# Chunked attention on one core: the second head's normalisation on GpSimd, its copy out of PSUM on VectorE

## The chip, the cores and the metric

The kernel runs on one core of a Trainium2 chip. The metric is the device time of one execution in microseconds, lower is better. Of the core's engines, TensorE (PE) multiplies matrices and transposes by a matmul, VectorE (DVE) and ScalarE (ACT) work on tiles of 128 partitions in SBUF or in the matmul banks (PSUM), GpSimd (POOL) works on SBUF, and SyncE (SP) issues most DMAs. They run unsynchronised but for semaphores.

## The reference

A first block of two layers and a second block of one, on 512 tokens of width 1024, in float32. Each layer has two feed-forward parts around a mixer. The odd layer's mixer is the one touched: attention in bands of chunks beside a pooling of several scales.

```python
def _chunk_band_attention(q, k, v, q_gain, k_gain, rel_bias):
    '''Each chunk attends to itself and LEFT_CHUNKS previous chunks. (B,S,512) each -> (B,S,512).'''
    ...
    scores = jnp.einsum('bclhd,bckhd->bhclk', q.astype(f32), kb.astype(f32)) * (ATT_HEAD_DIM ** -0.5)
    ...
    scores = jnp.where(valid[None, None, :, None, :], scores + bias[None, :, None], -jnp.inf)
    probs = jax.nn.softmax(scores, axis=-1)
    out = jnp.einsum('bhclk,bckhd->bclhd', probs, vb.astype(f32))
```

There are 8 heads of 64, chunks of 64 tokens and 8 chunks to the left, so with 512 tokens a query sees all keys up to the end of its own chunk.

## The kernel before, in words

Most of the time goes into dense products whose weights are split into a high and a low part (ScalarE copies the high part, line 242, VectorE subtracts the low one, line 248) and multiplied in three matmuls (lines 294 to 296 and their like). Each stage is written by hand: for every engine a block with its instructions in order, and semaphores between them. Between two stages all engines meet at a barrier. GpSimd clears the semaphores of stages gone by behind such a barrier (line 164), before it enters its own block of the next stage, if it has one.

`chunk_attend` (line 2530 on) is one such stage. It goes through n = 16 steps, a step being a pair of heads c (the first on partitions 0 to 63, the second on 64 to 127 of the operands) and a block t of 128 queries. The width of a step is (t + 1) x 128 keys. The steps of the first pair stand in the order t = 0, 1, 2, 3, those of the other three pairs in the order 3, 1, 2, 0: widths 512, 256, 384, 128, which makes a round of four steps. For each step and head:

- TensorE makes the scores in PSUM banks 0 to 3 (`scores`, line 2568).
- VectorE adds the bias, writes them to the tile `ca_sc` (three buffers) and takes the maximum (line 2667), and negates the maxima of both heads (line 2671).
- ScalarE takes the exponential in place and its sum (line 2641).
- VectorE takes the reciprocal of both sums (line 2675) and multiplies each head's exponentials by its own (line 2679). Semaphore `normed` counts these.
- TensorE transposes the probabilities in blocks of 128 into bank 4 (first head) or 5 (second head) (`turn`, line 2577).
- ScalarE copies each bank to the tile `ca_pt` (two buffers, line 2636). Semaphore `copied` counts these.
- TensorE multiplies with the values (`weigh`, line 2589).

The engines run ahead of each other: in its turn k TensorE does the scores of step k, the turns of step k - 2 and the weighting of step k - 3. A bank is turned into again when its copy of the step before is done. VectorE in its turn k does the maxima of step k, then the reciprocal and products of step k - 1. GpSimd has no block in this stage. At the end of each pair of heads its output goes out in two parts (lines 2652 and 2697), and in the last turns the pooling's products (line 2599) and the first matmuls of the next stage follow (line 354 on).

Of the kernel before, what the change touches and what calls it, by code (L numbers as in the profile page):

```python
# [19 lines left out]
ALU = mybir.AluOpType  # L20
ACT = mybir.ActivationFunctionType
# [2509 lines left out]
def chunk_attend(co, QK, V, BIAS, M, POOLED, PW, cols, nxt):  # L2531
# [7 lines left out]
    nc = co.nc  # L2539
    order = [(0, 1, 2, 3)] + 3 * [(3, 1, 2, 0)]  # L2540
    steps = [(c, t) for c in range(4) for t in order[c]]
    n = len(steps)
    with ExitStack() as ctx:
        SC = co.sb("ca_sc", [P, 3, 2, S], ctx=ctx)
        PT = co.sb("ca_pt", [P, 2, 2, S], ctx=ctx)
        ST = co.sb("ca_st", [P, 3, 4, 2], ctx=ctx)
        T = [co.RS, co.SS]
        (scored, biased, negated, powered, inverted, normed, turned, copied, weighted, out_hi, out_lo, pooled, scaled,
         rounded, parted) = (co.sem(f"ca_{s}") for s in (
            "scored", "biased", "negated", "powered", "inverted", "normed", "turned", "copied", "weighted", "out_hi",  # L2550
            "out_lo", "pooled", "scaled", "rounded", "parted"))
        block = ctx.enter_context(co.block())
        width = lambda k: (steps[k][1] + 1) * P

        @block.sync
        def _(sp):
            co.load_second(sp, nxt)

        @block.tensor
        def _(pe):  # L2560
            def scores(k):
                c, t = steps[k]
                w = width(k)
                if k >= 2:
                    pe.wait_ge(biased, 2 * (k - 2) + 2)
                for s in range(2):
                    r = HD * s
                    nc.tensor.matmul(co.PS[:, 2 * (k % 2) + s, 0:w], QK[r:r + HD, c, t * P:(t + 1) * P],
                                     QK[r:r + HD, 4 + c, 0:w], start=True, stop=True).then_inc(scored, 1)

            def turn(k):
                for s in range(2):
                    pe.wait_ge(normed, 2 * k + s + 1)
                    if k >= 1:
                        pe.wait_ge(copied, 2 * (k - 1) + s + 1)
                    for j in range(steps[k][1] + 1):
                        m = nc.tensor.transpose(co.PS[:, 4 + s, j * P:(j + 1) * P], SC[:, k % 3, s, j * P:(j + 1) * P],
                                                co.ident)
                    m.then_inc(turned, 1)

            def weigh(k):
                c, t = steps[k]
                pe.wait_ge(copied, 2 * k + 2)
                if k % TT == 0 and c >= 2:
                    pe.wait_ge(out_lo, c - 1)
                for j in range(t + 1):
                    for s in range(2):
                        h = 2 * c + s
                        m = nc.tensor.matmul(co.PS[HD * s:HD * s + HD, 6 + c % 2, t * P:(t + 1) * P],
                                             V[:, j, h * HD:(h + 1) * HD], PT[:, k % 2, s, j * P:(j + 1) * P],  # L2590
                                             start=j == 0, stop=j == t)
                m.then_inc(weighted, 1)

            def pooled_half(g):
                if g >= 2:
                    pe.wait_ge(scaled, g - 1)
                else:
                    pe.wait_ge(biased, 2 * n)
                nc.tensor.matmul(co.PS[:, 2 + g % 2, :], PW[:, g, :], POOLED[:, g, :], start=True, stop=True).then_inc(pooled, 1)
            def bank_read(pe, bank):  # L2600
                if bank == 2:
                    pe.wait_ge(scaled, 3)
                else:
                    pe.wait_ge(biased, 2 * n)
            for k in range(n + 3):
                if k < n:
                    scores(k)
                if 2 <= k < n + 2:
                    turn(k - 2)
                if k >= n + 1:  # L2610
                    for g in (2 * (k - n - 1), 2 * (k - n - 1) + 1):
                        pooled_half(g)
                if k >= 3:
                    weigh(k - 3)
                if k == n + 1:
                    pe.wait_ge(out_lo, 3)
                    co.begin_unit(pe, nxt, 0, (0, 1, 2), bank_read, last=False)
            pe.wait_ge(parted, 2)
            co.begin_unit(pe, nxt, 0, (4, 5), first=False, last=False)
            pe.wait_ge(parted, 4)  # L2620
            co.begin_unit(pe, nxt, 0, (6, 7), first=False, last=False)
            pe.wait_ge(out_lo, 4)
            co.begin_unit(pe, nxt, 0, (3,), first=False)
            for j in range(1, RAW - 1):
                co.begin_unit(pe, nxt, j, range(DC), bank_read)

        @block.scalar
        def _(act):
            for k in range(n + 3):
                if 2 <= k < n + 2:  # L2630
                    w = width(k - 2)
                    if k >= 4:
                        act.wait_ge(weighted, k - 3)
                    for s in range(2):
                        act.wait_ge(turned, 2 * (k - 2) + s + 1)
                        nc.scalar.activation(PT[:, k % 2, s, 0:w], co.PS[:, 4 + s, 0:w], ACT.Copy).then_inc(copied, 1)
                if k < n:
                    w = width(k)
                    act.wait_ge(negated, k + 1)
                    for s in range(2):  # L2640
                        nc.scalar.activation(SC[:, k % 3, s, 0:w], SC[:, k % 3, s, 0:w], ACT.Exp,
                                             bias=ST[:, k % 3, 1, s:s + 1], accum_out=ST[:, k % 3, 2, s:s + 1]).then_inc(powered, 1)
                if k == SPLIT_STEP:
                    co.split_hi(act, nxt, 0, 1)
                if k >= n + 1:
                    for g in (2 * (k - n - 1), 2 * (k - n - 1) + 1):
                        act.wait_ge(scaled, g + 1)
                        nc.scalar.activation(M[0][:, 4 + g, :], T[g % 2][:], ACT.Copy).then_inc(rounded, 1)
                if k >= 3 and (k - 3) % TT == TT - 1:
                    c = steps[k - 3][0]  # L2650
                    act.wait_ge(weighted, k - 2)
                    nc.scalar.activation(M[0][:, c, :], co.PS[:, 6 + c % 2, :], ACT.Copy).then_inc(out_hi, 1)
            for j in range(SPLIT, RAW):
                co.split_hi(act, nxt, 0, j)

        @block.vector
        def _(dve):
            v = nc.vector
            for k in range(n + 3):
                if k < n:  # L2660
                    c, t = steps[k]
                    w = width(k)
# [9 lines left out]
                if 1 <= k < n + 1:  # L2672
                    b = (k - 1) % 3
                    dve.wait_ge(powered, 2 * k)
                    v.reciprocal(ST[:, b, 3, :], ST[:, b, 2, :]).then_inc(inverted, 1)
                    dve.wait_ge(inverted, k)
                    w = width(k - 1)
                    for s in range(2):
                        v.tensor_scalar(SC[:, b, s, 0:w], SC[:, b, s, 0:w], ST[:, b, 3, s:s + 1], None,
                                        ALU.mult).then_inc(normed, 1)  # L2680
                if k == SPLIT_STEP + 1:
                    co.split_lo(dve, nxt, 0, 1)
                if k >= n + 1:
# [723 lines left out]
```

## Time and profile before

| | |
|---|---|
| median of 3 runs | 2734.49 us (2733.83 to 2734.65) |
| profiled execution | 2734.27 us, span from first to last instruction 2732.5 us |
| TensorE busy | 2696.5 us, 99% of the span |
| VectorE busy | 1402.7 us, 51% |
| ScalarE busy | 963.4 us, 35% |
| GpSimd busy | 208.1 us, 8% |
| mean granted TensorE clock | 0.999 |

The stage of the change begins at the barrier at about 1413.5 us and its last steps end at about 1456 us. TensorE's busy time counts from the start of a matmul to an end that is modelled, and consecutive matmuls overlap in it; the distance from one start to the next says what a matmul costs in a dense row. "PEld" is its weight loader, which may be idle while a matmul runs.

### The profile page before, as it was taken

To read this page: it belongs to the slowest core of one execution; us is meant where nothing else is said; L and a number is where in the kernel's file an instruction comes from. 1 tells how busy PE (TensorE), PEld (TensorE's weight loads), DVE (VectorE), ACT (ScalarE), POOL (GpSimd) and SP (SyncE) were. 2 spreads that over 40 slices of the span, in tenths; PEclk is the share of its full clock that TensorE was granted. 3 is DMA by queue.
4 is the path that set the end of the run, shared out by engine and by line. 5 is a ranking of instruction groups with operands and counts; after the bars stand their busy time and mean duration, and the time that the engine had idled before them with its cause. 6 is when DMAs were issued, how large, how long until landed. Compare 5 with 4: busy or idle time off the path is not lost. (4 is left out here: it accounts for less than half of the span.)

```text
span 2732.5 us, 33671 instructions
## 1 busy us (share of the span) xinstructions
PE 2696.5 (99%) x12904; PEld 2209.0 (81%) x12904; DVE 1402.7 (51%) x1806; ACT 963.4 (35%) x1346; POOL 208.1 (8%) x220
## 2 busy tenths in 40 slices
PE   8999999999999999999999999999999999999998
PEld 7888888788888888888877888888888777788887
DVE  6676236754443254442585544423998535633334
ACT  5433224643332233322245333222223642433213
POOL 2001013010000000000301000000000000300003
PEclk9999999999999999999999999999999999999999
DMA  4334236132233222232311222333442024222331
GB/s 161 123 129 170 97 108 185 51 138 99 94 104 108 81 92 100 92 111 91 118 62 62 100 92 100 112 111 106 149 135 78 33 73 139 81 93 99 104 106 52
DMA packets 77680, 282.74 MB, mean 103 GB/s; under 512 B 10240, under 2 KB 10880, under 8 KB 76816
## 3 DMA queue, kind: packets, MB, share of 16 engines
q1 hardware_dynamic: 66672, 248.50, 26.9%
q0 software_dynamic: 6304, 26.65, 3.0%
q10 hardware_dynamic: 4608, 6.30, 0.9%
q8 instruction: 62, 1.02, 0.2%
q14 instruction: 34, 0.28, 0.0%
HBM read 261.22 MB, written 13.89 MB: 101 GB/s over the span
## 5 line engine op out<-in xcount | busy, mean ns | idle before, releaser
L248 DVE TENSOR_TENSOR wl<-raw,wh 128x1024 fp32r<-128x1024 f32 (+3 forms) x435 | 562.7, 1293 | 1062.2 <-ACT wh L242 1061.1
L242 ACT ACTIVATE wh<-raw 128x1024 fp32r<-128x1024 f32 (+3 forms) x436 | 480.0, 1101 | 1093.2 <-PE PS L296 905.7
L294 PE MATMUL PS<-Hh,wl 128*128 128x512 f32 x2154 | 843.2, 391 | 1.7 <-DVEq L1493 0.5
L295 PE MATMUL PS<-Hh,wh 128*128 128x512 f32 x2154 | 838.2, 389 | 0.0
L296 PE MATMUL PS<-Hl,wh 128*128 128x512 f32 x2154 | 838.2, 389 | 0.0
L294 PEld LDWEIGHTS PS<-Hh,wl 128*128 128x128 f32 x2154 | 404.4, 188 | 89.9 <-issue 4.5
L295 PEld LDWEIGHTS PS<-Hh,wh 128*128 128x128 f32 x2154 | 404.4, 188 | 85.0 <-issue 1.9
L296 PEld LDWEIGHTS PS<-Hl,wh 128*128 128x128 f32 x2154 | 404.3, 188 | 83.9
L294 PE MATMUL PS<-ffn_gh,wl 128*128 128x512 f32 x880 | 342.7, 389 | 0.0
L296 PE MATMUL PS<-ffn_gl,wh 128*128 128x512 f32 x880 | 342.3, 389 | 0.0
L295 PE MATMUL PS<-ffn_gh,wh 128*128 128x512 f32 x880 | 342.3, 389 | 0.0
L294 PEld LDWEIGHTS PS<-ffn_gh,wl 128*128 128x128 f32 x880 | 165.2, 188 | 34.7 <-issue 0.2
L296 PEld LDWEIGHTS PS<-ffn_gl,wh 128*128 128x128 f32 x880 | 165.2, 188 | 34.4
L295 PEld LDWEIGHTS PS<-ffn_gh,wh 128*128 128x128 f32 x880 | 165.2, 188 | 34.2 <-issue 0.2
L1009 DVE TENSOR_TENSOR ffn_gl<-ffn_t,ffn_gh 128x512 f32 (+1 forms) x110 | 76.4, 694 | 93.1 <-ACT ffn_gh L972 93.1
L966 ACT ACTIVATE ffn_sg<-ffn_sg 128x512 f32<-128x512 f32 x88 | 55.7, 633 | 160.8 <-DVE ffn_sg L998 160.8
L972 ACT ACTIVATE ffn_gh<-ffn_t 128x512 f32 (+1 forms) x110 | 69.5, 632 | 109.9 <-DVE ffn_t L1003 77.3
L354 PE MATMUL PS<-Hh,wl 128*128 128x512 f32 x222 | 90.8, 409 | 10.5 <-DVE Hl L1229 8.0
L596 POOL TENSOR_TENSOR SS<-SS,ffn_sg 128x512 f32<-128x512 f32 x24 | 30.7, 1281 | 797.1 <-ACT ffn_sg L578 797.1
L355 PE MATMUL PS<-Hh,wh 128*128 128x512 f32 x222 | 87.4, 394 | 0.0
L356 PE MATMUL PS<-Hl,wh 128*128 128x512 f32 x222 | 87.3, 393 | 0.0
L2923 DVE SCALAR_TENSOR_TENSOR X<-conv_u,cols,X 128x512 f32<-128x512 f32 x124 | 85.0, 744 | 0.0
(495 smaller groups left out, 2533.9 us busy)
## 6 DMA issues: line engine op xcount, KB each, us to landing
raw<-in_gu SPq DMA_DIRECT2D x220, 512.0 KB, 3.6
raw<-in_dn SPq DMA_DIRECT2D x80, 704.0 KB, 4.0
raw<-in_hin SPq DMA_DIRECT2D x44, 512.0 KB, 3.6
raw<-in_oin SPq DMA_DIRECT2D x16, 512.0 KB, 3.6
raw<-in_hin_gate SPq DMA_DIRECT2D x16, 512.0 KB, 3.6
X<-QKV ACTq DMA_DIRECT2D x96, 64.0 KB, 2.0
kept_x<-X POOLq DMA_DIRECT2D x16, 256.0 KB, 3.6
raw<-in_eout SPq DMA_DIRECT2D x8, 512.0 KB, 3.7
```

The costliest lines, as they stand in the source:

```text
L242: self.nc.scalar.activation(self.wh[j % SPLIT][:, 0:kw], self.raw[j][:, 0:kw], ACT.Copy).then_inc(self.hi_ready, 1)
L248: self.nc.vector.tensor_sub(self.wl[j % SPLIT][:, 0:kw], self.raw[j][:, 0:kw], self.wh[j % SPLIT][:, 0:kw].bitcast(F32)).then_inc(self.lo_ ...
L294: self.nc.tensor.matmul(out, wl, xh[:, at, :], start=first, stop=False)
L295: self.nc.tensor.matmul(out, wh, xh[:, at, :], start=False, stop=False)
L296: done = self.nc.tensor.matmul(out, wh, xl[:, at, :], start=False, stop=last)
L354: self.nc.tensor.matmul(out, wl, xh[:, at, :], start=start, stop=False)
L355: self.nc.tensor.matmul(out, wh, xh[:, at, :], start=False, stop=False)
L356: done = self.nc.tensor.matmul(out, wh, xl[:, at, :], start=False, stop=stop)
L966: nc.scalar.activation(SG[:, c], SG[:, c], ACT.Silu).then_inc(gated, 1)
L972: nc.scalar.activation(one(Gh, n), T[:, c], ACT.Copy).then_inc(rounded, 1)
L1009: nc.vector.tensor_sub(one(Gl, n), T[:, c], one(Gh, n).bitcast(F32)).then_inc(g_ready, 1)
L2923: self.co.nc.vector.scalar_tensor_tensor(self.CV[:, n, :], self.U[:, n, tap:tap + S], self.co.cols[:, k:k + 1], self.CV[:, n, :], ALU.mult ...
```

## The change

In `chunk_attend`, three pieces of work of the second head change hands:

- the product of its exponentials with the reciprocal sum goes from VectorE (line 2679) to GpSimd, which gets a block in this stage with 16 such instructions;
- the copy of its turned probabilities from bank 5 to `ca_pt` goes from ScalarE (line 2636) to VectorE, where it stands behind the first head's product;
- `normed` and `copied` become two semaphores each, one per head, so the stage has 17 semaphores where it had 15.

```diff
+        normed = [co.sem(f"ca_normed{s}") for s in range(2)]
+        copied = [co.sem(f"ca_copied{s}") for s in range(2)]
...
+        @block.gpsimd
+        def _(pool):
+            for k in range(n):
+                b, w = k % 3, width(k)
+                pool.wait_ge(inverted, k + 1)
+                nc.gpsimd.tensor_scalar(SC[:, b, 1, 0:w], SC[:, b, 1, 0:w], ST[:, b, 3, 1:2], None,
+                                        ALU.mult).then_inc(normed[1], 1)
...
             def turn(k):
                 for s in range(2):
-                    pe.wait_ge(normed, 2 * k + s + 1)
+                    pe.wait_ge(normed[s], k + 1)
                     if k >= 1:
-                        pe.wait_ge(copied, 2 * (k - 1) + s + 1)
+                        pe.wait_ge(copied[s], k)
...
             def weigh(k):
-                pe.wait_ge(copied, 2 * k + 2)
+                for s in range(2):
+                    pe.wait_ge(copied[s], k + 1)
...
         def _(act):
-                    for s in range(2):
-                        act.wait_ge(turned, 2 * (k - 2) + s + 1)
-                        nc.scalar.activation(PT[:, k % 2, s, 0:w], co.PS[:, 4 + s, 0:w], ACT.Copy).then_inc(copied, 1)
+                    act.wait_ge(turned, 2 * (k - 2) + 1)
+                    nc.scalar.activation(PT[:, k % 2, 0, 0:w], co.PS[:, 4, 0:w], ACT.Copy).then_inc(copied[0], 1)
...
         def _(dve):
-                    for s in range(2):
-                        v.tensor_scalar(SC[:, b, s, 0:w], SC[:, b, s, 0:w], ST[:, b, 3, s:s + 1], None,
-                                        ALU.mult).then_inc(normed, 1)
+                    v.tensor_scalar(SC[:, b, 0, 0:w], SC[:, b, 0, 0:w], ST[:, b, 3, 0:1], None,
+                                    ALU.mult).then_inc(normed[0], 1)
+                if 2 <= k < n + 2:
+                    w = width(k - 2)
+                    if k >= 4:
+                        dve.wait_ge(weighted, k - 3)
+                    dve.wait_ge(turned, 2 * (k - 2) + 2)
+                    v.tensor_copy(PT[:, k % 2, 1, 0:w], co.PS[:, 5, 0:w]).then_inc(copied[1], 1)
```

Line numbers in the rows of order are each kernel's own. VectorE's queue before, in the first pair of heads, from the negated maxima of one step to those of the next (2667 are the maxima and their read-out, 2671 the negation, 2675 the reciprocal, 2679 the two heads' products):

```order
L2671 TENSOR_SCALAR ca_st<-ca_st 128x2
L2675 RECIPROCAL ca_st<-ca_st 128x2
L2679 TENSOR_SCALAR ca_sc<-ca_sc,ca_st 128x384 x2
L2667 ISA ca_sc,ca_st<-PS,BIAS 128x512
L2667 ISA ca_st 128x1
L2667 ISA ca_sc,ca_st<-PS,BIAS 128x512
L2667 ISA ca_st 128x1
L2671 TENSOR_SCALAR ca_st<-ca_st 128x2
```

The same place on VectorE after the change (2677, 2681, 2685 and 2688 answer to 2667, 2671, 2675 and 2679; 2695 is the copy out of bank 5):

```order
L2681 TENSOR_SCALAR ca_st<-ca_st 128x2
L2685 RECIPROCAL ca_st<-ca_st 128x2
L2688 TENSOR_SCALAR ca_sc<-ca_sc,ca_st 128x384
L2695 COPY ca_pt<-PS 128x256
L2677 ISA ca_sc,ca_st<-PS,BIAS 128x512
L2677 ISA ca_st 128x1
L2677 ISA ca_sc,ca_st<-PS,BIAS 128x512
L2677 ISA ca_st 128x1
L2681 TENSOR_SCALAR ca_st<-ca_st 128x2
```

One product of a step is left, and the copy of the step before it (256 keys beside 384) stands between that product and the maxima of the step after.

GpSimd's queue at the entry of the stage, as a difference (L164 are the semaphore clears, L2561 the entry of its new block, L1047 that of the next stage):

```order
-L164 ISA x63
+L164 ISA x48
+L2561 UNCONDITIONAL_BRANCH
+L2566 TENSOR_SCALAR ca_sc<-ca_sc,ca_st 128x128
+L2566 TENSOR_SCALAR ca_sc<-ca_sc,ca_st 128x256
+L2566 TENSOR_SCALAR ca_sc<-ca_sc,ca_st 128x384
+L2566 TENSOR_SCALAR ca_sc<-ca_sc,ca_st 128x512 x2
```

Before, 48 clears stood behind the barrier at the stage's beginning and 15 behind the one at its end, with nothing between them. Now the 48 stand ahead of the 16 products, and 17 follow at the end.

## Rows read from the trace of the kernel before

**Rows 1.** Busy time by stretch, inside the stage; the first line names the columns

```profile
core 0: us, PE busy (x) PEld busy (x) DVE busy (x) ACT busy (x) POOL busy (x), PEclk, DMA share, GB/s
1430.00:1440.00 10.00, 9.85 (x85) 6.00 (x82) 8.49 (x35) 7.96 (x27) 0.00 (x0) 1.00 0.00 0
```

**Rows 2.** Waits in the stage: who for whom, us in total, times, longest

```profile
PEld PS L2577 <- DVE ca_sc L2679: 8.7, 15, 1.3
```

**Rows 3.** Timeline of TensorE, one round: start us, us, operation, count, idle before

```profile
1429.47 1.13 PE L2568 MATMUL PS<-QK 64*128 64x512 f32 x4
1430.53 0.88 PE L2577 MATMUL PS<-ident,ca_sc 128*128 128x128 f32 x6
1431.34 0.66 PE L2589 MATMUL PS<-ca_pt,V 128*64 128x128 f32 x8
1431.92 0.70 PE L2568 MATMUL PS<-QK 64*128 64x256 f32 x4
1432.70 0.53 PE L2577 MATMUL PS<-ident,ca_sc 128*128 128x128 f32 x2
1433.15 0.88 PE L2589 MATMUL PS<-ca_pt,V 128*64 128x128 f32 x12
1433.96 0.92 PE L2568 MATMUL PS<-QK 64*128 64x384 f32 x4
1434.81 1.09 PE L2577 MATMUL PS<-ident,ca_sc 128*128 128x128 f32 x8
1435.83 0.44 PE L2589 MATMUL PS<-ca_pt,V 128*64 128x128 f32 x4
1436.20 0.49 PE L2568 MATMUL PS<-QK 64*128 64x128 f32 x4
1436.77 0.70 PE L2577 MATMUL PS<-ident,ca_sc 128*128 128x128 f32 x4
1437.41 1.09 PE L2589 MATMUL PS<-ca_pt,V 128*64 128x128 f32 x16
1438.43 1.13 PE L2568 MATMUL PS<-QK 64*128 64x512 f32 x4
```

**Rows 4.** Groups by form: VectorE's products, count, busy us, mean ns, idle before

```profile
L2679 DVE TENSOR_SCALAR ca_sc<-ca_sc,ca_st 128x512 f32<-128x512 f32 x8 | 3.5, 484 | 0.1
...
L2679 DVE TENSOR_SCALAR ca_sc<-ca_sc,ca_st 128x128 f32<-128x128 f32 x8 | 1.9, 284 | 0.1
```

**Rows 5.** Lines by source: VectorE's copies out of PSUM, ns least/median/most

```profile
L3035 DVE COPY QKV<-PS x2: 681/687/693, 2102.9 to 2103.5; 128x512 f32<-128x512 f32 x2
...
L1539 DVE COPY AC<-PS x1: 183/183/183, 464.0 to 464.0; 128x32 f32<-128x32 f32 x1
```

**Rows 6.** Lines by source: GpSimd's tensor_scalar, ns least/median/most

```profile
L2411 POOL TENSOR_SCALAR POOLED<-POOLED x4: 1450/1452/1469, 1343.8 to 1369.5; 128x496 f32<-128x496 f32 x4
...
L1320 POOL TENSOR_SCALAR SZ<-SZ x7: 287/289/732, 428.7 to 435.1; 128x32 f32<-128x32 f32 x7
```

**Rows 7.** Timelines of VectorE and GpSimd elsewhere, two places where they meet

```profile
575.59 1.22 DVE L248 TENSOR_TENSOR wl<-raw,wh 128x1024 fp32r<-128x1024 f32 x1 [1.23 <-ACT wh L242]
...
575.59 2.37 POOL L596 TENSOR_TENSOR SS<-SS,res_sq 128x512 f32<-128x512 f32 x1
...
1371.07 1.30 POOL L2412 TENSOR_TENSOR POOLED<-POOLED,UU 128x512 f32<-128x512 f32 x1
...
1371.42 2.02 DVE L248 TENSOR_TENSOR wl<-raw,wh 128x1024 fp32r<-128x1024 f32 x1
```

**Rows 8.** Timeline of VectorE in the round: reciprocals at two steps, one pair of products

```profile
1432.16 0.16 DVE L2675 RECIPROCAL ca_st<-ca_st 128x2 f32<-128x2 f32 x1
...
1433.84 0.17 DVE L2675 RECIPROCAL ca_st<-ca_st 128x2 f32<-128x2 f32 x1
1434.04 0.89 DVE L2679 TENSOR_SCALAR ca_sc<-ca_sc,ca_st 128x512 f32<-128x512 f32 x2
```

**Rows 9.** The stage's start: GpSimd's semaphore clears, and TensorE's first turns

```profile
L164 POOLq EVENT_SEMAPHORE_RANGE_CLEAR  x48: 44/44/44, 1413.6 to 1417.2; - x48
...
1416.36 0.53 PE L2577 MATMUL PS<-ident,ca_sc 128*128 128x128 f32 x2 [0.73 <-DVE ca_sc L2679]
```

More of the change, by code:

```diff
@@ L2547, in chunk_attend @@
         T = [co.RS, co.SS]
-        (scored, biased, negated, powered, inverted, normed, turned, copied, weighted, out_hi, out_lo, pooled, scaled,
+        (scored, biased, negated, powered, inverted, turned, weighted, out_hi, out_lo, pooled, scaled,
          rounded, parted) = (co.sem(f"ca_{s}") for s in (
-            "scored", "biased", "negated", "powered", "inverted", "normed", "turned", "copied", "weighted", "out_hi",
+            "scored", "biased", "negated", "powered", "inverted", "turned", "weighted", "out_hi",
             "out_lo", "pooled", "scaled", "rounded", "parted"))
+        normed = [co.sem(f"ca_normed{s}") for s in range(2)]
+        copied = [co.sem(f"ca_copied{s}") for s in range(2)]
         block = ctx.enter_context(co.block())
```

## The prediction

> **What bounds the kernel now.** I read the page's busy shares first: TensorE 99% of the span, VectorE 51%, ScalarE 35%, GpSimd 8%. The change lives in one stage of some 45 us, so I looked next at that stage by windows [rows 1]: in 10 us TensorE is busy 9.85, VectorE 8.49, ScalarE 7.96, GpSimd 0, at the full granted clock of 2.4 GHz (1.00). Three engines are nearly full, and the busy TensorE is a modelled figure, so it does not say who leads. The waits do [rows 2]: 8.7 us of idle on TensorE's weight loader end with VectorE's products (line 2679), longest 1.3 us. Most of that idle lies under matmuls still running; what truly stops TensorE must be counted from the spacing of its groups.
>
> That is the third view, the timeline of one round of four steps (widths 512, 256, 384, 128 keys) [rows 3]. The round takes 1438.43 - 1429.47 = 8.96 us. Unwaited costs, start to next start: scores 1.06 (512) and 0.85 (384), so 0.21 per 128 keys and 0.64 and 0.42 for the narrow ones; turns 0.81 for 6 transposes and 1.02 for 8, so 0.59 for 4 and 0.37 for 2; weighting 0.58, 0.81, 0.37, 1.02 for 8, 12, 4, 16 matmuls. Sum: 2.97 + 2.79 + 2.78 = 8.54. So TensorE waits 0.42 in the round; it is the bound, and VectorE's chain, scores to product, follows closely. Three such rounds hold 1.3 us of waits; the same count of the timeline's other steps gives about 1.2 us before step 4 and 0.4 in steps 4 to 7, and some 0.5 at the end: about 3.4 us of real waiting in the stage. No relief of the other engines can give back more.
>
> **The change, part by part.** (a) ScalarE loses 16 copies of the second head's turned scores. It is not what TensorE waits for (0.42 a round ends with VectorE's products), so I price it at nothing; the exponentials can start earlier, which VectorE, itself the later one, does not use. Bounds: 0 to -1.3 us.
>
> (b) VectorE loses one product per step and gains one copy out of PSUM. The products took 484 ns at 512 keys and 284 at 128 [rows 4], 0.48 + 0.42 + 0.35 + 0.28 = 1.53 us a round. The copy at 512 columns is 687 ns and at 32 columns 183 [rows 5], 1.05 ns a column: 0.69 + 0.55 + 0.42 + 0.28 = 1.94. VectorE's share of a round rises from 0.849 x 8.96 = 7.6 to 8.0 of 8.96 us: fuller, not yet the bound by sum. But the copy is a new wait in VectorE's row of work: it stands after the remaining product and before the next step's reductions, and holds them until TensorE has turned the second head. TensorE in turn may not turn the second head of the next step until that copy has emptied the bank.
>
> (c) GpSimd takes the second head's product. A tensor_scalar there took 1450 ns at 496 columns and 287 at 32 when undisturbed [rows 6], so 2.51 ns a column against 0.52 on VectorE: 1.49 us at 512 keys, 1.17, 0.85 and 0.53 at 384, 256 and 128. The row takes a number as its factor and the new instruction a column of values; VectorE pays about 60 ns for that, so I take the rows' durations and keep +0.3 us for the upper end, and -0.2 for the lower.
>
> (d) Both products are released by the same reciprocal. What happens when VectorE and GpSimd want SBUF together is in [rows 7]: released in the same instant, 575.59, VectorE's took 1.22 us, its usual time, and GpSimd's took 2.37, where 1.30 is what such a one takes alone (third row): it ran after VectorE's, with some 0.13 of its start beside it. Started second, VectorE is the one who pays: GpSimd at 1371.07 for 1.30, VectorE at 1371.42 for 2.02 instead of 1.22. Those are VectorE instructions with two SBUF operands; none in this trace shows VectorE's one-operand product beside GpSimd. Bounds for the hold: none to the whole product, and I take the whole, with VectorE first, as in the nearest row. The Trainium skill, page "SBUF — State Buffer", section "Who interferes with whom", says that a VectorE tensor_scalar in its two-port form and any GpSimd instruction exclude each other for the whole instruction, whoever issued first. By that rule the sum is the 3.3 us below, without it 2.6; the trace agrees in so far as [rows 7] show exclusion and [rows 4] a product at 0.52 ns a column, half of the copy's 1.05, as a form with two ports would have it.
>
> Now the second head's product at 512 keys, from the reciprocal's start. Before: 0.20 + 0.89 for the pair [rows 8] = 1.09. After: 0.20 + 0.48 held + 1.36 = 2.04. In the round shown the reciprocal starts at 1433.84, so the product comes at 1435.88, with 0.06 to the release 1435.94; TensorE wants it at 1434.81 + 0.50 = 1435.31. It waits 0.63, where it had 0.32 to spare. At 128 keys: reciprocal at 1432.16, VectorE's product 0.20 + 0.20, then the copy of the 384-key step 0.55 and 0.06: the bank is free at 1433.17, wanted at 1432.70 + 0.19 = 1432.89, a wait of 0.28. At 384 keys the product (1.66 after its reciprocal) still hides.
>
> Each stall also moves what follows, so I stepped through all 16 steps with these durations, each engine in its new order and each wait honoured. On the order before, this walk gives a round of 8.90 (the trace: 8.96); on the new order 9.60, with TensorE waiting 0.49 for the 512-key product, 0.10 for the 256-key one, and 0.44 at the 128-key step (0.30 of it for the copy). So +0.7 a round.
>
> (e) The start. GpSimd clears 48 semaphores after the barrier, until 1417.2 [rows 9], and only then enters the new block; idle before, this cost nobody. Its first product starts at about 1417.4 and ends at 1417.95. TensorE turned the second head of step 0 at 1416.56 (0.2 into the group at 1416.36) and will at 1418.04, 1.5 us later. As it waited for VectorE shortly after anyway, 1.0 us is left at the scores of step 4. Bounds: 0.2 (were the clears free) to 1.5.
>
> Sum by the walk: start +1.0; steps 4 to 7, where wide products follow each other, +0.9; two rounds +0.7 each; the tail, which waits for the same pooled products as before, about 0: **+3.3 us**. The walk runs 0.06 a round short, so I say +3.5. The profiled execution took 2734.27 us around a span of 2732.5; the median of the runs is 2734.49, 0.2 more. 2734.49 + 3.5 = **2738.0 us**. Behind the stage TensorE runs without gaps, so the shift is kept whole.
>
> **The rivals.**
> A. It gets faster or stays: the relieved ScalarE and the half-relieved pair of products let TensorE run dry of waits. For it: the 8.7 us of loader idle that end with VectorE's products, and TensorE at 98% in the stage, where only 3.4 us can be had. Against: that product is not removed but made 0.95 us later at 512 keys. It would give up to -2 us: 2732.5 to 2735. Chance 0.12.
>
> B. GpSimd wins the port. If its product is already streaming when VectorE's is issued, the first head waits for the second: VectorE's product starts 1.5 us later, its copy, reductions and next reciprocal with it. It decides from the point at which GpSimd starts before VectorE; the walk with that order loses 2.5 us by step 4 and 3.5 us in each round, +15 us: 2749.5. For it: VectorE at 1371.42 [rows 7]. Against: the tie at 575.59 went to VectorE, and here VectorE starts 0.03 us after its own reciprocal. The same page's rule, that issue order decides who blocks, would give this time if GpSimd is the earlier; the trace shows no such pair of starts here. Chance 0.07.
>
> C. GpSimd's product costs more with a column as factor, or its start is later than I think: +0.3 us a product makes +5.3, +0.5 makes +6.7 (the walk), and a start 1 us later adds 1.0: 2739.5 to 2743. Chance 0.23.
>
> D. GpSimd's product is as quick as VectorE's in effect. The copy alone then costs +1.6: 2736. Chance 0.10, inside the main case's side of zero.
>
> Main case, +1.8 to +5: chance 0.48.
>
> **How the numbers follow.** The time is the main case's. The range: below it A leaves some 0.1 out, above it B and a little of C; 2735.3 to 2743. From 0.2% (5.5 us) a change of this kernel can be told from none. Faster by that much would need more than the 3.4 us that the stage holds: 0.02. Slower by it needs C's upper half or B: 0.25. The rest, 0.73, is within it, most of it on the slow side.
>
> **What would show it.** GpSimd in the stage: 16 tensor_scalar instructions, the first at 1417.3 to 1417.7, of some 1.85 us at 512 keys when the hold is counted in their time (1.5 if there is none), VectorE's own product staying at 0.48. TensorE's round 9.6 us, the second head's turns released by GpSimd at 512 keys and by the copy at the 128-key step, and the scores of step 4 near 1420.2. VectorE's copies 0.69 us at 512. I am wrong if the round stays at 9.0 (then the product hides and A or D holds), if VectorE's products grow beyond 1 us (B), or if GpSimd's exceed 2.1 us (C).

## The result, and the profile after

The changed kernel takes 2739.01 us (median of 20 runs, 2737.77 to 2743.78) against 2734.53 us of the kernel before (20 runs): +4.5 us, ratio 1.0017, 95% interval 1.0011 to 1.0023. The forecast was 2738.0 with a range to 2743.0. The profiled execution took 2738.76 us around a span of 2737.0.

The stage can be measured in the trace, from its first scores to the last of the next stage's products that wait for it. I measure every kernel below in that way, since the profiled executions reach this stage at times up to 1.4 us apart (1412.93 to 1414.36) for reasons that lie in other stages. Stations, in us from the stage's first scores:

| | scores of step 4 | of step 8 | of step 12 | first pooled product | end | stage against before |
|---|---|---|---|---|---|---|
| before | 5.52 | 15.82 | 24.78 | 35.98 | 46.39 | |
| after | 7.67 | 19.51 | 29.33 | 41.39 | 51.81 | +5.42 |

The stage lost 5.42 us. The profiled execution reached it at 1412.93 where before's did at 1413.65, and another 0.2 us was made up behind it, so its whole time is only 4.5 more. By stations: +2.15 up to step 4, +1.54 in steps 4 to 7, +0.86 in the round to step 12, +0.86 to the first pooled product, +0.01 behind it.

TensorE's timeline of the changed kernel, the start and one whole round, answers to [rows 3] (start us, us, operation, count, and the idle time before with what ended it; the round in [rows 3] began at 1429.47):

```profile
1412.93 1.98 PE L2578 MATMUL PS<-QK 64*128 64x128 f32 x12 [0.30 <-PEq L180]
1415.64 0.33 PE L2587 MATMUL PS<-ident,ca_sc 128*128 128x128 f32 x1 [0.73 <-DVE ca_sc L2688]
1417.39 0.33 PE L2587 MATMUL PS<-ident,ca_sc 128*128 128x128 f32 x1 [1.42 <-POOL ca_sc L2566]
1417.64 1.35 PE L2578 MATMUL PS<-QK 64*128 64x512 f32 x4
1418.92 1.11 PE L2587 MATMUL PS<-ident,ca_sc 128*128 128x128 f32 x4
...
1420.59 1.73 PE L2578 MATMUL PS<-QK 64*128 64x512 f32 x4
1422.25 0.88 PE L2587 MATMUL PS<-ident,ca_sc 128*128 128x128 f32 x6
...
1432.44 1.13 PE L2578 MATMUL PS<-QK 64*128 64x512 f32 x4
...
1434.89 0.70 PE L2578 MATMUL PS<-QK 64*128 64x256 f32 x4
1435.66 0.33 PE L2587 MATMUL PS<-ident,ca_sc 128*128 128x128 f32 x1
1436.22 0.30 PE L2587 MATMUL PS<-ident,ca_sc 128*128 128x128 f32 x1 [0.23 <-DVE ca_pt L2695]
1436.45 0.88 PE L2600 MATMUL PS<-ca_pt,V 128*64 128x128 f32 x12
...
1438.10 0.66 PE L2587 MATMUL PS<-ident,ca_sc 128*128 128x128 f32 x4
1439.03 0.66 PE L2587 MATMUL PS<-ident,ca_sc 128*128 128x128 f32 x4 [0.27 <-POOL ca_sc L2566]
1439.62 0.44 PE L2600 MATMUL PS<-ca_pt,V 128*64 128x128 f32 x4
...
1440.41 0.89 PE L2587 MATMUL PS<-ident,ca_sc 128*128 128x128 f32 x4
1441.23 1.09 PE L2600 MATMUL PS<-ca_pt,V 128*64 128x128 f32 x16
1442.25 1.13 PE L2578 MATMUL PS<-QK 64*128 64x512 f32 x4
```

The round is 1442.25 - 1432.44 = 9.81 us, 9.82 by the stations, where it was 8.96. Two idle times are printed, but the spacing shows four places. With the unwaited costs of the prediction (turns 0.37, 0.59, 1.02 for 2, 4, 8 transposes, scores of 256 keys 0.64): turns of the 128-key step 1436.45 - 1435.66 = 0.79, so 0.42 waited; turns at 512 keys 1439.62 - 1438.10 = 1.52, so 0.50; at 256 keys 1441.23 - 1440.41 = 0.82, so 0.23; and 0.13 behind the scores at 1434.89. Together 1.28, where the round before had 0.42.

At the start there is something else. Four scores of 512 keys take 1.06 us from start to start in a dense row; here they take 1418.92 - 1417.64 = 1.28 and 1422.25 - 1420.59 = 1.66. Busy time by stretch, with the granted clock as the column behind POOL, tells why; the last row answers to [rows 1]:

```profile
core 0: us, PE busy (x) PEld busy (x) DVE busy (x) ACT busy (x) POOL busy (x), PEclk, DMA share, GB/s
1412.00:1414.00 2.00, 1.57 (x16) 1.00 (x14) 1.06 (x6) 1.48 (x2) 0.00 (x0) 1.00 0.06 20
1414.00:1416.00 2.00, 1.23 (x5) 0.43 (x5) 1.85 (x11) 1.99 (x9) 0.00 (x0) 1.00 0.69 244
1416.00:1418.00 2.00, 0.61 (x3) 0.44 (x5) 1.37 (x8) 1.53 (x7) 1.34 (x2) 1.00 0.01 2
1418.00:1420.00 2.00, 2.00 (x10) 0.75 (x6) 0.91 (x4) 0.43 (x2) 0.24 (x1) 0.61 0.00 0
1420.00:1422.00 2.00, 2.00 (x9) 0.77 (x8) 1.43 (x6) 1.35 (x4) 1.19 (x1) 0.54 0.00 0
1422.00:1424.00 2.00, 2.00 (x20) 1.35 (x18) 1.50 (x6) 0.69 (x3) 0.28 (x1) 1.00 0.00 0
1430.00:1440.00 10.00, 9.42 (x86) 5.64 (x82) 8.41 (x35) 6.87 (x22) 5.29 (x5) 1.00 0.00 0
```

TensorE's granted clock fell to its lower level, 1.2 GHz, for 2 x (0.39 + 0.46) / 0.5 = 3.4 us. In a busy-share view this is invisible: TensorE counts 2.00 of 2.00 while it does half the work. In the kernel before it is 1.00 in the same stretch (rows in the last section), and here it is again from 1422 on.

The waits in the stage (who for whom, us in total, times, longest), where [rows 2] had 8.7 us of the loader's idle ended by VectorE:

```profile
PEld PS L2587 <- POOL ca_sc L2566: 5.4, 9, 1.6
...
PEld PS L2587 <- DVE ca_sc L2688: 4.1, 6, 1.3
```

The loader's wait has changed its address, and GpSimd now ends the larger part. Durations by form in the stage (count, busy us, mean ns), answering to [rows 4 to 6]:

```profile
L2566 POOL TENSOR_SCALAR ca_sc<-ca_sc,ca_st 128x512 f32<-128x512 f32 x4 | 7.4, 1856 | 4.1 <-DVE ca_st L2685 4.0
L2566 POOL TENSOR_SCALAR ca_sc<-ca_sc,ca_st 128x384 f32<-128x384 f32 x4 | 5.9, 1470 | 4.8 <-DVE ca_st L2685 4.8
L2566 POOL TENSOR_SCALAR ca_sc<-ca_sc,ca_st 128x256 f32<-128x256 f32 x4 | 4.2, 1041 | 3.4 <-DVE ca_st L2685 3.4
L2566 POOL TENSOR_SCALAR ca_sc<-ca_sc,ca_st 128x128 f32<-128x128 f32 x4 | 2.8, 690 | 49.2 <-remote 44.9 <-DVE ca_st L2685 4.3
...
L2695 DVE COPY ca_pt<-PS 128x512 f32<-128x512 f32 x4 | 2.7, 686 | 0.2 <-PE PS L2587 0.2
...
L2688 DVE TENSOR_SCALAR ca_sc<-ca_sc,ca_st 128x512 f32<-128x512 f32 x4 | 1.9, 486 | 0.2
```

GpSimd needs 1.86 us at 512 keys, VectorE's product beside it is as long as it was (486 against 484 ns), and the copy takes 0.69. The means at 256 and 128 keys contain the first two products, which met VectorE's in another order or not at all (0.92 and 0.68 us); the later ones take 1.08 and 0.69.

### The profile page after: what moved, and what is told of

It is laid out like the page before. It is cut to its first block and busy times, and to the rows that moved or that the text cites. A ratio compares the mean times of both kernels' runs of the same rounds, so it can differ in the third digit from the quotient of the medians.

```text
span 2737.0 us, 33701 instructions
## 1 busy us (share of the span) xinstructions
PE 2698.7 (99%) x12904; PEld 2209.2 (81%) x12904; DVE 1404.3 (51%) x1806; ACT 959.0 (35%) x1330; POOL 228.3 (8%) x236
## 3 DMA queue, kind: packets, MB, share of 16 engines
q8 instruction: 62, 1.02, 0.2%
```

## The experiments

Three questions: what the start costs and why (clears, clock), what the copy and the product each cost in the steady rounds, and whether GpSimd's time is its own or held back by VectorE. Experiments 1 to 4 shared 33 runs of the kernel before (median 2734.40 us), 5 to 8 another 33 (2733.97); each ran 11 times. The edits are against the changed kernel. All stations together, in us as above; whether the clock falls is read from the profiled execution:

| | step 4 | step 8 | step 12 | pooled | end | stage | clock falls | median us | ratio (95%) |
|---|---|---|---|---|---|---|---|---|---|
| 1 product only | 7.52 | 19.52 | 29.27 | 41.47 | 51.87 | +5.48 | yes | 2739.18 | 1.0018 (1.0009-1.0027) |
| 2 copy only | 5.78 | 17.04 | 27.19 | 39.57 | 49.99 | +3.60 | no | 2737.63 | 1.0012 (1.0003-1.0021) |
| 3 kept busy | 6.74 | 18.25 | 28.06 | 40.14 | 50.55 | +4.16 | no | 2737.86 | 1.0012 (1.0003-1.0021) |
| 4 first two on VectorE | 5.78 | 17.09 | 26.91 | 39.36 | 49.77 | +3.38 | no | 2738.06 | 1.0012 (1.0003-1.0021) |
| 5 clears left out | 5.84 | 17.09 | 26.91 | 38.98 | 49.39 | +3.00 | no | 2737.08 | 1.0011 (1.0002-1.0020) |
| 6 after the first head | 7.45 | 19.99 | 30.21 | 42.74 | 53.15 | +6.76 | yes | 2739.94 | 1.0021 (1.0012-1.0030) |
| 7 no wide ones on GpSimd | 5.78 | 16.57 | 26.39 | 38.37 | 48.77 | +2.38 | no | 2736.54 | 1.0009 (1.0000-1.0018) |
| 8 narrow copies | 5.52 | 15.82 | 24.79 | 35.95 | 46.37 | -0.02 | no | 2734.03 | 0.9999 (0.9990-1.0008) |

The intervals of the ratios overlap for most pairs, so the separations rest on the stations, of one profiled execution each. How far these can be trusted shows where the code is equal: the round from step 8 to 12 is 9.81 or 9.82 us in the changed kernel and in experiments 3, 4 and 5. But from step 12 to the first pooled product experiment 4 takes 12.45 us and experiment 5, with the same instructions there, 12.08: the maxima of step 12 start 1.64 us after their scores and not 1.27, once, and nothing in that trace says why. So a difference of 0.4 us in one place can be chance. For the fall of the clock there is a second sign: of every run the mean granted clock is on record, and it is 0.998 in 6 of 20 runs of the changed kernel, 6 of 11 of experiment 1 and 7 of 11 of experiment 6, and in none of the 66 runs of the other six experiments.

**Experiment 1, the product alone.** ScalarE copies both heads again, GpSimd keeps the product.

```diff
         def _(act):
+                    act.wait_ge(turned, 2 * (k - 2) + 2)
+                    nc.scalar.activation(PT[:, k % 2, 1, 0:w], co.PS[:, 5, 0:w], ACT.Copy).then_inc(copied[1], 1)
         def _(dve):
-                    v.tensor_copy(PT[:, k % 2, 1, 0:w], co.PS[:, 5, 0:w]).then_inc(copied[1], 1)
```

> GpSimd makes all 16 second-head products as in the changed kernel, but ScalarE keeps copying both heads. Theory (three costs: GpSimd's late start with a drop of TensorE's clock behind it, the late 512-key product, the copy in VectorE's loop): the start and the wide products stay, the copy's part goes. Steps 0 to 3 cost +2.1 us as in the changed kernel, with a stretch of 3.4 us at half clock; rounds of about 9.6; in all +3.5 to +4.5 us against before. Rival (the copy on VectorE alone makes the loss, the product hides): +1 us or less, rounds at 9.0.

Measured: the stage is +5.48, as long as with both parts, and the median +4.8. The round is 9.75 (step 8 to 12), the start +2.00 with the clock down. The expectation was wrong in one part: the copy's share was to go (rounds of 9.6, +3.5 to +4.5), but the round is only 0.07 shorter with the copy back on ScalarE. At the 128-key step of the changed kernel the copy that empties the bank and GpSimd's product end at the same moment, 1436.08 and 1436.07:

```profile
1435.38 0.69 POOL L2566 TENSOR_SCALAR ca_sc<-ca_sc,ca_st 128x128 f32<-128x128 f32 x1 [2.07 <-DVE ca_st L2685]
1435.53 0.55 DVE L2695 COPY ca_pt<-PS 128x384 f32<-128x384 f32 x1
```

Without the copy TensorE still waits there for the product, 0.35 us for 0.42 by the spacing, and the 0.50 at 512 keys stays as it was. What ScalarE's relief is worth by itself this run does not say, since VectorE's load changes with it.

**Experiment 2, the copy alone.** Both products are VectorE's again, its copy stays.

```diff
-        @block.gpsimd
-        def _(pool):
...
+                    v.tensor_scalar(SC[:, b, 1, 0:w], SC[:, b, 1, 0:w], ST[:, b, 3, 1:2], None,
+                                    ALU.mult).then_inc(normed[1], 1)
```

> VectorE makes both products as before and also copies the second head out of PSUM; GpSimd has no block. Theory: no start cost and no clock drop (scores of step 4 at most 0.3 us late in the stage), but VectorE has 1.9 us more per round and becomes the bound: rounds of about 9.9 to 10.0, in all +2.5 to +3.5 us. Rival (GpSimd's product makes the whole loss, the copy hides in VectorE's idle): 0 to +0.5 us, rounds at 9.0.

Measured: +3.60 in the stage and +3.2 in the median, near the theory; the rival is out. The round is 10.15, longer than with both parts. Its timeline shows the place, the turns of the second head in the 128-key and the 256-key step:

```profile
1435.16 0.30 PE L2579 MATMUL PS<-ident,ca_sc 128*128 128x128 f32 x1 [0.42 <-DVE ca_pt L2689]
...
1439.97 0.41 PE L2579 MATMUL PS<-ident,ca_sc 128*128 128x128 f32 x2 [0.51 <-DVE ca_pt L2689]
```

Line 2689 is the copy: TensorE stands twice a round until VectorE has emptied the bank. VectorE is busy 9.33 us of these 10.15 and waits for scores in 0.54 of them; before, it was busy 7.73 of 8.96. This is no test of the prediction's rival D (+1.6), in which VectorE makes one product a step and not two. The two parts don't add. Alone they cost 0.79 (9.75) and 1.19 (10.15) a round, together 0.86: where VectorE must copy, GpSimd's product takes work off a full engine and gives 0.33 back.

**Experiment 3, TensorE kept busy.** Matmuls whose result nobody reads fill TensorE's wait for the first product of GpSimd; all else is the changed kernel.

```diff
             def turn(k):
                 for s in range(2):
+                    if k == 0 and s == 1:
+                        co.idle_products(7, 6)
                     pe.wait_ge(normed[s], k + 1)
```

> The changed kernel with six dummy 128x128 matmuls into an unused bank on TensorE, between the two turns of step 0, where it waits 1.4 us for GpSimd's first product. If the granted clock fell because of that wait: it stays at 1.00 all through the stage, the scores of step 4 come 1.1 us earlier, and the time is 0.9 to 1.2 us below the changed kernel's: +3.3 to +3.6 against before. Rival (the drop comes of something else, as GpSimd's or VectorE's load): the drop stays and the time is that of the changed kernel, +4.5.

Measured: the clock stays at 1.00 where it had fallen (windows with the columns of above),

```profile
1418.00:1420.00 2.00, 2.00 (x15) 0.90 (x14) 1.04 (x4) 0.79 (x3) 0.56 (x1) 1.00 0.00 0
1420.00:1422.00 2.00, 1.67 (x9) 0.60 (x7) 1.93 (x7) 1.20 (x3) 1.07 (x1) 1.00 0.00 0
```

and the stage is 5.42 - 4.16 = 1.26 us shorter, 0.93 of it by step 4 and 0.33 by step 8; from there on the stations run in parallel. The median, 2737.86, is 1.15 under the changed kernel's (1.0 if each is taken against the kernel before of its own set). So the idle TensorE brought the clock down, and that is worth 1.26 us here, not the 1.7 that 3.4 us at half speed would be; in part because TensorE, at full clock again, waits at other places (by its timeline 0.23 and 0.56 us at the turns of the 384-key step, step 2).

**Experiment 4, the first two products on VectorE.** GpSimd takes the second head from step 2 on.

```diff
+                if k >= 2:
+                    pool.wait_ge(inverted, k + 1)
+                    nc.gpsimd.tensor_scalar(SC[:, b, 1, 0:w], SC[:, b, 1, 0:w], ST[:, b, 3, 1:2], None,
+                                            ALU.mult).then_inc(normed[1], 1)
...
+                    if not ((k - 1) >= 2):
+                        v.tensor_scalar(SC[:, b, 1, 0:w], SC[:, b, 1, 0:w], ST[:, b, 3, 1:2], None,
+                                        ALU.mult).then_inc(normed[1], 1)
```

> The changed kernel, but VectorE makes the second head's products of steps 0 and 1; GpSimd begins with step 2. Theory (the start costs 2.1 us, about 1.0 by GpSimd's late entry behind its 48 semaphore clears and 1.1 by the clock that falls behind it): no wait at step 0, clock 1.00, scores of step 4 at most 0.3 us late, rounds unchanged at 9.8: +2.4 to +3.3 us against before. Rival (the start costs nothing that isn't paid anyway later): +4.5.

Measured: step 4 at 5.78, only 0.26 behind the kernel before, the clock at 1.00. Of the +2.15 at the start 1.89 is gone; the rounds are unmoved (9.82). The median is less clear than the stations, 2738.06 (2736.05 to 2738.72): +3.7, above the +2.4 to +3.3 expected. Of the stage's +3.38, 0.38 is the single delay behind step 12 named above; without it the stage would be +3.00, as in experiment 5.

**Experiment 5, the clears left out at this stage's entry.** GpSimd's 48 semaphore clears don't stand ahead of its first product but follow at the next stage's entry; all 16 products stay there.

```diff
-        co.begin()
+        co.begin(f.__name__ != "chunk_attend")
...
-    def begin(self):
+    def begin(self, clear=True):
+        if not clear:
+            self.stage_sems = StageSems()
+            return
```

> The changed kernel with GpSimd's 48 semaphore clears put off to the next stage's beginning, so that it can start the product of step 0 as soon as the reciprocal is there. If the clears are what holds the start: GpSimd's first product begins at its reciprocal (2.2 us into the stage's matmuls), TensorE waits under 0.4 us more at step 0 than before, clock 1.00, scores of step 4 at most 0.4 us late; stage 3.2 to 3.5 us longer than before, time +2.4 to +3.4. Rival (entering a block of its own is what costs, whatever stands ahead): start and clock as in the changed kernel, +4.5 to +5.4.

Measured: GpSimd's first product starts 2.44 us into the stage (which began at 1413.16) and not 3.73 (1416.66 - 1412.93), and it is released by the reciprocal:

```profile
1415.60 0.69 POOL L2569 TENSOR_SCALAR ca_sc<-ca_sc,ca_st 128x128 f32<-128x128 f32 x1 [43.71 <-DVE ca_st L2688]
```

Step 4 comes at 5.84, the clock does not fall; the stage is +3.00, a little under the 3.2 expected, and the median +3.1, as expected. So the queue of clears [rows 9] costs 1.83 us by step 4, its consequence on the clock included; GpSimd as the executor of the first two narrow products costs 0.06 more than VectorE (5.84 against 5.78).

**Experiment 6, GpSimd behind the first head.** Its product waits for VectorE's, so the two never overlap.

```diff
-                pool.wait_ge(inverted, k + 1)
+                pool.wait_ge(normed[0], k + 1)
```

> The changed kernel, but GpSimd waits for VectorE's product of the first head instead of the reciprocal, so that the two products never overlap. If in the changed kernel GpSimd is held for the whole of VectorE's product: its instructions now take 1.45 to 1.55 us at 512 keys instead of 1.86, and end no more than 0.15 us later; stage 0 to 0.8 us longer than the changed kernel's. Rival (the two share the memory at a lower rate): the instructions shrink too, but end 0.3 us or more later, VectorE's product at 0.49 gets shorter, and the stage grows by 1.3 us or more.

Measured: alone, the product takes

```profile
L2566 POOL TENSOR_SCALAR ca_sc<-ca_sc,ca_st 128x512 f32<-128x512 f32 x4 | 6.3, 1565 | 5.7 <-DVE ca_sc L2688 5.7
L2566 POOL TENSOR_SCALAR ca_sc<-ca_sc,ca_st 128x384 f32<-128x384 f32 x4 | 5.0, 1245 | 5.8 <-DVE ca_sc L2688 5.8
...
1436.54 0.61 POOL L2566 TENSOR_SCALAR ca_sc<-ca_sc,ca_st 128x128 f32<-128x128 f32 x1 [2.39 <-DVE ca_sc L2688]
```

and 0.93 us at 256 keys. That is 0.29, 0.22, 0.16 and 0.09 us less from 512 to 128 keys than in the changed kernel, where VectorE's products beside it take 0.49, 0.42, 0.35 and 0.29. At every width GpSimd loses VectorE's product less 0.20 us. Of these 0.20, 0.06 pass before GpSimd starts, and 0.14 of its own time lies beside VectorE's product: at 512 keys it ends 1.43 us behind VectorE's and takes 1.57 alone. The rest of VectorE's product it waits. The kernel is nevertheless slower, +1.34 in the stage and 10.22 a round. The 512-key product of the changed kernel and of this one, from the reciprocal on, first the changed kernel:

```profile
1436.87 0.16 DVE L2685 RECIPROCAL ca_st<-ca_st 128x2 f32<-128x2 f32 x1
1437.06 0.49 DVE L2688 TENSOR_SCALAR ca_sc<-ca_sc,ca_st 128x512 f32<-128x512 f32 x1
...
1437.12 1.86 POOL L2566 TENSOR_SCALAR ca_sc<-ca_sc,ca_st 128x512 f32<-128x512 f32 x1 [1.05 <-DVE ca_st L2685]
```

and experiment 6:

```profile
1437.70 0.16 DVE L2685 RECIPROCAL ca_st<-ca_st 128x2 f32<-128x2 f32 x1
1437.90 0.49 DVE L2688 TENSOR_SCALAR ca_sc<-ca_sc,ca_st 128x512 f32<-128x512 f32 x1
...
1438.48 1.56 POOL L2566 TENSOR_SCALAR ca_sc<-ca_sc,ca_st 128x512 f32<-128x512 f32 x1 [1.33 <-DVE ca_sc L2688]
```

The product ends 2.11 us after the reciprocal's start in the one and 1438.48 + 1.56 - 1437.70 = 2.34 in the other. So the overlap saves 0.23: the 0.14 beside VectorE, and 0.09 from the end of VectorE's product (1438.39) to GpSimd's start (1438.48), which the wait for its semaphore adds. Every GpSimd product later by that makes the round 0.40 longer. The theory is met in part: GpSimd's instructions shrink as it says, but they end 0.23 later and not within 0.15, and the stage's +1.34 is the rival's size. What the rival needs is missing: VectorE's product takes 0.49 alone as beside GpSimd's, so the two don't share at a lower rate.

**Experiment 7, no wide products on GpSimd.** It takes the second head only where there are fewer than 512 keys and from step 2 on; VectorE does the others.

```diff
+        gp = lambda k: k >= 2 and width(k) < S
...
+                if gp(k):
+                    pool.wait_ge(inverted, k + 1)
...
+                    if not gp(k - 1):
+                        v.tensor_scalar(SC[:, b, 1, 0:w], SC[:, b, 1, 0:w], ST[:, b, 3, 1:2], None,
+                                        ALU.mult).then_inc(normed_v, 1)
```

> GpSimd makes the second head's product only from step 2 on and only at widths under 512 keys; VectorE makes the others; VectorE copies the second head at every step. Against the run in which VectorE makes only the first two. If the 512-key product is what TensorE waits for besides the copy: about 0.5 us less in the stage, +2.4 to +3.1 against before. Rival (VectorE's load is the bound, as its copy alone costs 3.6 us in the stage): the product given back to VectorE lengthens it by 0.4 us at each of four steps, and the stage is as long as with the first two alone or longer.

Measured: +2.38 in the stage, 1.00 less than experiment 4, of which 0.52 comes in steps 4 to 7 and 0.47 behind step 12. Of the latter 0.38 is experiment 4's single delay; against experiment 5 the stage is 0.62 shorter, near the 0.5 expected. The round from step 8 is 9.82, unmoved: the wait at 512 keys is gone (its 8 transposes run as one group), but the one at 256 keys has grown from 0.23 to 0.57 by the spacing, and 0.16 has come in behind the scores ahead of it,

```profile
1437.51 0.44 PE L2595 MATMUL PS<-ident,ca_sc 128*128 128x128 f32 x2
1438.30 0.44 PE L2595 MATMUL PS<-ident,ca_sc 128*128 128x128 f32 x2 [0.35 <-POOL ca_sc L2569]
```

The wait at the 128-key step is 0.42 as before. So the wide product alone does not set the steady round; which loop of VectorE's copies and GpSimd's narrow products does, these rows don't settle. The 0.50 removed at one step came back at the next.

**Experiment 8, narrow copies only.** No GpSimd; VectorE does both products and copies the second head only at 128 and 256 keys, ScalarE at 384 and 512.

```diff
+        cv = lambda k: k >= 2 and width(k) <= 2 * P
...
+                    if not cv(k - 2):
+                        act.wait_ge(turned, 2 * (k - 2) + 2)
+                        nc.scalar.activation(PT[:, k % 2, 1, 0:w], co.PS[:, 5, 0:w], ACT.Copy).then_inc(copied[1], 1)
...
-                if 2 <= k < n + 2:
+                if 2 <= k < n + 2 and cv(k - 2):
```

> Both products on VectorE as before, GpSimd without a block; VectorE copies the second head out of PSUM only at 128 and 256 keys from step 2 on, ScalarE all else. If the copy costs by its length in VectorE's full queue: 0.28 and 0.42 us of copies where VectorE has idle time cost nothing, and the stage is that of before within 0.3 us. Rival (each copy costs by its place, since it makes VectorE wait for TensorE's turn): half of the loss of all copies, +1.5 to +2 us.

Measured: -0.02 in the stage, round 8.97, 2734.03 against 2733.97 us. Two of four copies a round on VectorE are free, and relieve ScalarE without any gain. So a copy does not cost by standing in that place. That the wide ones, 0.69 and 0.55 us in front of the next maxima, are what costs in experiment 2 is argued and not shown: no run has the wide ones alone, and it may be the sum that counts (VectorE is busy 8.17 of 8.97 us here, 9.33 of 10.15 there). Of all variants this is the only one whose stage is no longer than before's, and it is not faster either.

## Why the prediction was right, and where it was not

The direction, the place and the order of size were right: +3.5 forecast, +4.5 measured, inside the range. Step by step:

- **(a) ScalarE's relief is worth nothing**: right as far as it was tested. Experiment 8 relieves it of the narrow copies and gains nothing. Experiment 1 gives all copies back to it and the stage stays (+5.48 against +5.42), but VectorE's load changes with that.
- **(b) The copy is 0.69 us at 512 keys, and a new wait at the 128-key step**: right by rows; that wait was put at 0.44 and is 0.55, 0.42 at the turns and 0.13 behind the scores before them. The walk laid 0.30 of it to the copy. GpSimd's product ends at the same moment, and nearly all of the wait stays without the copy (experiment 1). Rival D's price of +1.6 was not tested: in experiment 2 (+3.60) VectorE has both products beside the copies, by the prediction's numbers 7.6 + 1.94 = 9.5 us of work in a round of 10.15.
- **(c) GpSimd's product**: 1.49, 1.17, 0.85 and 0.53 forecast, 1.57, 1.25, 0.93 and 0.61 measured alone (experiment 6). That is 0.08 us more at every width. The column as factor is the likely cause, like the 60 ns that VectorE pays for it, which the prediction kept for the upper end; no run changes the factor alone.
- **(d) The hold**: right. The row of the instruction came out at 1.86 against 1.85, with VectorE first and unhurt at 486 ns. The agreement hides two small errors of opposite sign: the product itself is 0.08 longer, and it starts 0.06 after VectorE's, which its row does not count. The 0.13 beside VectorE is right (0.14). GpSimd did run first in two places (rows in the last section): VectorE's product lost nothing in the one, and a small VectorE instruction 0.1 us in the other. The Trainium skill, page "SBUF — State Buffer", section "Who interferes with whom", has the later one blocked for the whole of the other's instruction. The trace agrees on who waits, less the 0.14 us at the start, but for the row at 1416.66, where VectorE's product came 0.18 us later and was not blocked.
- **Rounds**: +0.7 forecast, +0.86 measured, twice. The walk had 0.49 of waits at 512 keys, 0.10 at 256 and 0.44 at 128; measured are 0.50, 0.23 and 0.55 (0.42 + 0.13). The 0.08 of (c) goes the right way for this; no run isolates it.
- **Steps 4 to 7**: +0.9 forecast, +1.54 measured, of which experiment 3 gives 0.33 to the slow clock: 11.51 - 10.30 = 1.21 without it.
- **(e) The start**, the step that failed. The clears do hold the first product: it began 3.73 us into the stage, 3.75 was forecast (1417.4 - 1413.65), and experiment 5 shows that they alone do. The second head of step 0 was to be turned 1.5 us later and was, by 1.55 (4.46 us into the stage for 2.91), with TensorE idle for 1.42 before it. But "1.0 us is left at the scores of step 4" was 2.15. At full clock it is 1.22 (experiment 3); the other 0.93 is TensorE at 1.2 GHz for 3.4 us after that wait, of which the prediction has no word. It had read a clock of 1.00 in [rows 1] and carried it over to a stretch that the change itself thins out.
- **The tail**: 0 forecast, 0.01 measured.

In sum the walk's 3.3 stands against 4.16 at full clock (start +0.22, steps 4 to 7 +0.3, rounds +0.34), and the clock adds 1.26: 5.42. That is above the main case's +5. The whole time moved by +4.5 because the profiled execution reached the stage 0.72 us earlier and made up 0.2 behind it, where the prediction kept the shift whole; to that extent the closeness of the forecast is luck. The median of the 20 runs moved by +4.5 too, and the stage doesn't explain why; over the experiments the median moved between 0.8 us less and 0.3 more than the stage (+6.0 and +6.76 in the sixth, +3.7 and +3.38 in the fourth); the stations are from one execution each, and where the rest goes stays open.

The rivals: A (no slower) is out, since the whole interval of the ratio, 1.0011 to 1.0023, lies above 1. B did not happen. C's mechanism, a dearer product, is there at a quarter of its smallest size, 0.08 for 0.3. D is out by GpSimd's own 1.57 us for VectorE's 0.49, and by experiment 1, where the product alone costs 0.79 us a round.

Why no variant was faster: the 3.4 us of waits in the stage before lie in rounds of 8.96 us in which VectorE is already busy 7.73 and ScalarE 7.30. A part moved off ScalarE takes nothing off VectorE, and what GpSimd takes off VectorE comes back a microsecond later at 512 keys (2.11 after the reciprocal's start, where it was 1.09). Whether another order of the steps could use the relieved ScalarE was not tried.

## What to carry to other kernels

Before an engine that was idle is given its first work in a stage, read what already stands in its queue there: 48 semaphore clears were free as long as GpSimd had nothing to do, and cost 1.83 us at once when it had. Price a stall of TensorE in a thin stretch with the clock as well as with its length, and check the granted clock in windows of 2 us around it, since the busy share shows nothing. And price each half of a swap alone with the whole loop of the fullest engine stepped through: here the product alone cost 0.79 us a round, the copy alone 1.19, and both together 0.86.

## What the runs showed of the hardware

**The clock fell after a wait of 1.4 us.** TensorE was busy 1.57, 1.23 and 0.61 of 2 us in the three windows before it; its granted clock went from 2.4 to 1.2 GHz at about 1418.4 (by the 0.61 of that window), one microsecond after it had work again, and stayed there for 3.4 us while TensorE was full. In the kernel before the same stretch was busy 1.70, 1.49 and 1.58, and another stage of it has a longer wait, 1.69 us between dense matmuls, with the clock at 1.00 through and behind it:

```profile
528.00:530.00 2.00, 0.31 (x3) 0.16 (x4) 1.90 (x4) 1.98 (x5) 0.00 (x0) 1.00 0.00 0
530.00:532.00 2.00, 2.00 (x38) 2.00 (x39) 1.97 (x3) 1.47 (x3) 0.00 (x0) 1.00 0.00 0
...
1412.00:1414.00 2.00, 1.70 (x19) 1.54 (x19) 1.24 (x2) 1.48 (x3) 0.00 (x0) 1.00 0.00 0
1414.00:1416.00 2.00, 1.49 (x11) 0.47 (x8) 1.69 (x11) 1.99 (x6) 0.00 (x0) 1.00 0.66 217
1416.00:1418.00 2.00, 1.58 (x6) 0.58 (x6) 1.91 (x9) 1.51 (x7) 0.00 (x0) 1.00 0.13 49
```

So the longest wait of a trace that shows no fall is no safe bound for one that comes in a thin stretch. It fell in all three kernels with the late first product and TensorE idle (after, experiments 1 and 6), and in neither the kernel before nor the other six experiments.

**When one reciprocal releases both products, GpSimd waits for VectorE**, which starts 0.06 us earlier, in all four widths: VectorE's durations are unchanged (486 ns at 512 keys), and all but 0.14 us of GpSimd's work lies behind VectorE's end. The earlier start does not always decide. GpSimd's first product ran from 1416.66 to 1417.33, and VectorE's came 0.18 us after its start and took its usual 0.35; GpSimd's took 0.68 where it takes 0.61 alone. And GpSimd's product of 1424.14 held VectorE's negation, which took 0.27 us for 0.17 and ended with it (0.50 at the same place in experiment 6). The first row holds the products of steps 0 and 1 together:

```profile
1416.66 1.58 POOL L2566 TENSOR_SCALAR ca_sc<-ca_sc,ca_st 128x128 f32<-128x128 f32 x2 [44.93 <-remote]
...
1416.84 0.35 DVE L2688 TENSOR_SCALAR ca_sc<-ca_sc,ca_st 128x256 f32<-128x256 f32 x1
...
1425.75 0.27 DVE L2681 TENSOR_SCALAR ca_st<-ca_st 128x2 f32<-128x2 f32 x1
```

**GpSimd's tensor_scalar with a column as factor** costs 0.29 us and 2.50 ns a column in f32, from 606 ns at 128 and 1565 at 512 columns alone (experiment 6, without its first two); 925 at 256 and 1245 at 384 lie on that line. With a number as factor [rows 6] a column costs the same, 2.51 ns, and the start 0.08 us less.
